# Eleven pairs of seven products in the second input projection

## The reference

```
z = rms_norm(h, norm1_g) @ w_in            # 1024 x 3584: 28 column tiles of 128
cb, cc, ch = split(z[..., :1536], 3)       # convolution, 4 tiles of 128 each
rq, rk, rv, rg = split(z[..., 1536:], 4)   # retention, 4 heads of 128 each
y_conv = group_rms_norm(cb * causal_dwconv3(cc * ch, conv_w), conv_norm_g, 8)
q = rotary(rq); k = rotary(rk) * 128 ** -0.5
o = chunkwise_retention(q, k, v)           # chunks of 128 tokens, a state from chunk to chunk
y_ret = group_rms_norm(o, ret_norm_g, 4) * silu(rg)
h = h + concat([y_conv, y_ret]) @ w_out
```

## Time and profile before

| | |
|---|---|
| median of 3 runs (lowest, highest) | 2289.05 us (2288.67, 2289.07) |
| time of the profiled execution | 2289.21 us |
| its span, first to last instruction | 2287.4 us |
| mean granted clock of PE | 0.998 |
| PE busy | 2270.7 us, 99% |
| DVE busy | 1598.9 us, 70% |
| POOL busy | 1109.2 us, 48% |
| ACT busy | 818.0 us, 36% |

### The profile page before, as it was taken

One profiled execution on the slowest core, in us unless ns is written; L12 is line 12 of the kernel. 1 busy time (PEld: TensorE's weight loads), 2 busy tenths in 40 slices (PEclk: granted clock), 3 DMA queues, 4 the chain that ended last, 5 costly groups with the idle time before them and its releaser, 6 DMA issues.

```text
span 2287.4 us, 32269 instructions
## 1 busy us (share of the span) xinstructions
PE 2270.7 (99%) x10812; PEld 1896.3 (83%) x10812; DVE 1598.9 (70%) x2259; ACT 818.0 (36%) x1336; POOL 1109.2 (48%) x1252
## 2 busy tenths in 40 slices
PE   9999999999999999999999999999999999999998
PEld 7888888888888888888888888888888888888886
DVE  7666666756778777876666666555687877787766
ACT  5233333334634444444430002002453444344432
POOL 4332323234666566656543333443556665666561
PEclk9999999999999999999999999999999999999999
DMA  4110101124264546454312111111335545554553
GB/s 157 37 37 29 34 31 33 33 77 144 92 213 150 181 172 214 147 183 172 120 49 81 38 37 43 43 45 47 103 136 184 194 146 191 183 190 149 194 195 136
DMA packets 56966, 265.40 MB, mean 116 GB/s; under 512 B 6960, under 2 KB 8112, under 8 KB 39472
## 3 DMA queue, kind: packets, MB, share of 16 engines
q1 hardware_dynamic: 56304, 262.12, 33.5%
q10 hardware_dynamic: 576, 2.13, 0.3%
HBM read 206.55 MB, written 57.67 MB: 116 GB/s over the span
## 4 chain that ended last, share of the span: by engine, by line
PE 94%; DVE 3%; DVEq 1%; ACT 1%; issue 0%; DMA 0%; POOL 0%; SPq 0%; ACTq 0%; POOLq 0%
PE prod_ps L752 13%; PE prod_ps L754 13%; PE prod_ps L753 13%; PE prod_ps L1018 8%; PE prod_ps L1019 8%; PE prod_ps L1020 8%; PE side_ps L1018 7%; PE side_ps L1019 7%; PE side_ps L1020 7%; PE side_ps L893 2%; PE side_ps L805 2%; PE side_ps L811 1%; PE side_ps L821 1%; PE side_ps L831 1%; PE side_ps L823 1%; PE prod_ps L1052 1%
## 5 line engine op out<-in xcount | busy, mean ns | idle before, releaser
L752 PE MATMUL prod_ps<-operand_hi,w_hi 128*128 128x512 f32 x1336 | 532.0, 398 | 0.9 <-DVE operand_lo L1452 0.3
L754 PE MATMUL prod_ps<-operand_hi,w_lo 128*128 128x512 f32 x1336 | 521.7, 390 | 0.0
L753 PE MATMUL prod_ps<-operand_lo,w_hi 128*128 128x512 f32 x1336 | 520.3, 389 | 0.0
L579 POOL CAST w_hi<-w_raw 128x1024 fp32r<-128x1024 f32 x81 | 86.7, 1071 | 655.2 <-PE prod_ps L754 630.9
L583 POOL TENSOR_TENSOR w_lo<-w_raw,w_hi 128x256 fp32r<-128x256 f32 x324 | 302.6, 964 | 6.5
L754 PEld LDWEIGHTS prod_ps<-operand_hi,w_lo 128*128 128x128 f32 x1336 | 250.7, 188 | 53.9
L752 PEld LDWEIGHTS prod_ps<-operand_hi,w_hi 128*128 128x128 f32 x1336 | 251.1, 188 | 51.7 <-issue 1.5
L753 PEld LDWEIGHTS prod_ps<-operand_lo,w_hi 128*128 128x128 f32 x1336 | 251.2, 188 | 49.0
L624 POOL TENSOR_TENSOR w_lo<-w_raw,w_hi 128x256 fp32r<-128x256 f32 x168 | 155.7, 947 | 128.2 <-ACT w_hi L2551 127.4
L624 POOL TENSOR_TENSOR w_lo<-w_s,w_hi 128x256 fp32r<-128x256 f32 x168 | 129.7, 775 | 142.8 <-ACT w_more_hi L2559 114.8
L1863 DVE TENSOR_TENSOR x_res<-prod_ps,x_res 128x512 f32<-128x512 f32 x130 | 89.0, 685 | 95.7 <-PE prod_ps L1020 95.6
(11 more groups left out here) (369 smaller groups left out, 5413.3 us busy)
## 6 DMA issues: line engine op xcount, KB each, us to landing
w_raw<-stream SPq DMA_DIRECT2D x202, 512.0 KB, 3.7
x_park<-x_res SPq DMA_DIRECT2D x45, 1024.0 KB, 8.0
x_res<-x_park SPq DMA_DIRECT2D x45, 1024.0 KB, 6.7
swapped<-op_park SPq DMA_DIRECT2D x39, 1024.0 KB, 5.0
op_park<-swapped SPq DMA_DIRECT2D x6, 1024.0 KB, 7.8
x_in<-x_t SPq DMA_DIRECT2D x16, 256.0 KB, 5.5
x_res<-x_t SPq DMA_DIRECT2D x8, 512.0 KB, 4.5
out_t<-x_res SPq DMA_DIRECT2D x16, 256.0 KB, 2.0
```

The costliest lines, as they stand in the source:

```text
L579: nc.gpsimd.tensor_copy(w_hi[:, slot], w_raw[:, slot]).then_inc(high_made, 1)
L752: nc.tensor.matmul(into, w_h, a_h, start=(k == 0), stop=False)
L753: nc.tensor.matmul(into, w_h, a_l, start=False, stop=False)
L754: last = nc.tensor.matmul(into, w_l, a_h, start=False, stop=(k == KT - 1))
```

## The change

Units `U_IN2`+6 to the last of the convolution, 22 of them, are taken in 11 pairs. A pair of units is two column blocks by two halves of tokens. Over inner tiles 0-3 its four outputs are made from seven products of sums (operands B11, B21, B22 and T1 to T4; weights A11, A12, A22 and S1 to S4) instead of eight; over inner tiles 4-7 they are made plainly (`plain`). The first six units stay as they were. All four banks of `prod_ps` serve a pair, in an order that `pair_banks` turns from pair to pair. ACT copies four intermediate values out of PSUM to `in_c`, and DVE adds them (`got`) before it goes on; three of the four evacuations then read `in_c` in SBUF. Slot 0 of the weights holds the part for seven products, slot 1 the plain part.

T2, T3, T4 and the further weight parts take the place of `x_res`. So `x_res` is scaled early (gain on ACT, factor on POOL for tiles 4, 5, 6, 7, 0, 1; tiles 2, 3 on DVE), written to DRAM (`end1_park`, four transfers of 1 MB) and read back at the output projection (eight of 512 KB). The operands T1 to T4 are made on DVE and ACT in heads 0 and 1 and in pair 0. The copies of v, o and back move from DVE to ACT. The retention's loop is written out; its steps stand at named places of the pairs.

```diff
+            def split_paired(j):
+
+                u = U_PAIRED + 2 * j
+                raw, s12_raw = w_raw[:, 0], s12[0]
+
+                def behind(event):
+                    if j:
+                        pool.wait_ge(in_prod, 7 * (j - 1) + event)
+
+                def low(dst, src, high, highs):
+                    pool.wait_ge(in_high, 4 * j + highs)
+                    return nc.gpsimd.tensor_tensor(dst, src, high.bitcast(F32), ALU.subtract)
+
+                def upper(i):
+                    ks = slice(4 * i, 4 * i + 4)
+                    nc.gpsimd.tensor_copy(w_hi[:, 1, ks], w_raw[:, 1, ks]).then_inc(in_up_high, 1)
+                    pool.wait_ge(in_up_high, 2 * j + i + 1)
+                    for ks in (slice(4 * i, 4 * i + 2), slice(4 * i + 2, 4 * i + 4)):
+                        last = nc.gpsimd.tensor_tensor(w_lo[:, 1, ks], w_raw[:, 1, ks], w_hi[:, 1, ks].bitcast(F32),
+                                                       ALU.subtract)
+                    return last
+
+                pool.wait_ge(w_landed[0], u * 8 + 16)
+                if j:
+                    behind(4)
+                else:
+                    pool.wait_ge(prod, 2 * u - 2)
+                nc.gpsimd.tensor_tensor(s12_raw[:, 0:2], raw[:, 4:6], raw[:, 6:8], ALU.add)
+                pool.drain()
+                nc.gpsimd.tensor_tensor(s12_raw[:, 2:4], s12_raw[:, 0:2], raw[:, 0:2], ALU.subtract).then_inc(in_sum, 1)
+                low(w_lo[:, 0, 0:2], raw[:, 0:2], w_hi[:, 0, 0:2], 1).then_inc(in_parts, 1)
+                low(w_lo[:, 0, 2:4], raw[:, 2:4], w_hi[:, 0, 2:4], 1).then_inc(in_parts, 1)
+                low(w_lo[:, 0, 4:6], s12_raw[:, 0:2], w_hi[:, 0, 4:6], 2).then_inc(in_parts, 1)
+                behind(5)
+                if not j:
+                    pool.wait_ge(prod, 2 * u)
+                pool.wait_ge(w_landed[1], u * 8 + 16)
+                upper(0).then_inc(in_parts, 1)
+                behind(6)
+                if not j:
+                    pool.wait_ge(end1_parked[1], 16)
+                nc.gpsimd.tensor_tensor(in_s34[:, 0:2], raw[:, 0:2], raw[:, 4:6], ALU.subtract)
+                nc.gpsimd.tensor_tensor(in_s34[:, 2:4], raw[:, 2:4], s12_raw[:, 2:4], ALU.subtract).then_inc(in_sum, 1)
+                low(w_lo[:, 0, 6:8], s12_raw[:, 2:4], w_hi[:, 0, 6:8], 2).then_inc(in_parts, 1)
+                for ks in (slice(0, 2), slice(2, 4)):
+                    part = low(in_s34_lo[:, ks], in_s34[:, ks], in_more_hi[:, ks], 3)
+                part.then_inc(in_parts, 1)
+                low(in_a22_lo[:], raw[:, 6:8], in_more_hi[:, 4:6], 4).then_inc(w_split, 1)
+                pool.wait_ge(prod, 2 * u)
+                upper(1).then_inc(w_split, 1)
+                pool.sem_inc(high_made, 2)
...
+                part(1)
+                free(n_u)
+                seventh(b_u, A11, B11, True).then_inc(in_prod, 1)
+                part(3)
+                free(n_v)
+                sum_ready(1)
+                seventh(b_v, S1, T1, True).then_inc(in_prod, 1)
+                free(n_w)
+                seventh(b_w, A12, B21, True)
+                then("P2")
+                part(4)
+                plain(b_w, 0, 0, False).then_inc(in_prod, 1)
+                then("c11")
+                copied(1)
+                part(5)
+                sum_ready(2)
+                seventh(b_u, S2, T2, False).then_inc(in_prod, 1)
+                then("P6")
+                free(n_z)
+                plain(b_z, 0, 1, True)
+                part(6)
+                seventh(b_z, S4, B22, False).then_inc(in_prod, 1)
+                then("c12")
+                copied(3)
+                sum_ready(3)
+                seventh(b_u, S3, T3, False).then_inc(in_prod, 1)
+                then("P7")
+                pe.wait_ge(w_split, u + 2)
+                plain(b_v, 1, 1, False).then_inc(in_prod, 1)
+                then("c22")
+                copied(4)
+                sum_ready(4)
+                seventh(b_u, A22, T4, False).then_inc(prod, 2)
+                then("P4")
+                plain(b_u, 1, 0, False).then_inc(prod, 2)
+                then("c21")
...
+            paired(0, {"P2": old(1, "v"), "c11": old(1, "kv"), "c12": old(1, "o")})
+            paired(1, {"c11": new(2, "scores"), "c12": old(1, "back"), "c22": new(2, "k"), "c21": old(2, "v")})
+            paired(2, {"P2": old(2, "kv"), "c12": old(2, "o"), "P4": new(3, "scores")})
+            paired(3, {"P2": old(2, "back"), "c11": new(3, "k"), "c12": old(3, "v"), "c22": old(3, "kv")})
+            paired(4, {"P2": old(3, "o"), "P7": old(3, "back")})
...
+            def got(u, slot, half):
+
+
+                if not (isinstance(u, int) and U_PAIRED <= u < U_OUT2):
+                    wait_prod(u, half)
+                    return bank(slot, half), evac
+                j, odd = divmod(u - U_PAIRED, 2)
+                b_u, b_v, b_w, b_z = (prod_ps[:, n] for n in PAIR_BANKS[j])
+
+                def add(c, src):
+                    nc.vector.tensor_tensor(c[:], src, c[:], ALU.add).then_inc(evac, 1)
+                    dve.drain()
+                    return c[:], in_used
+
+                if not odd and half == 0:
+                    dve.wait_ge(in_copied, 4 * j + 1)
+                    dve.wait_ge(in_prod, 7 * j + 3)
+                    return add(in_c[0], b_w)
+                if not odd:
+                    dve.wait_ge(in_copied, 4 * j + 3)
+                    nc.vector.tensor_tensor(in_c[2][:], in_c[2][:], in_c[1][:], ALU.add)
+                    dve.drain()
+                    dve.wait_ge(in_prod, 7 * j + 5)
+                    return add(in_c[2], b_z)
+                if half == 1:
+                    dve.wait_ge(in_copied, 4 * j + 4)
+                    dve.wait_ge(in_prod, 7 * j + 7)
+                    return add(in_c[3], b_v)
+                dve.wait_ge(prod, 2 * u + 2)
+                return b_u, evac
...
+            def in_combine(op, m, half, other):
+
+                for kk in range(2):
+                    last = nc.vector.scalar_tensor_tensor(
+                        in_raw[op][:, kk], x_res[:, m + kk, tokens(half)], gain[:, G_END1_MIX2, m + kk:m + kk + 1],
+                        in_raw[other][:, kk], ALU.mult, ALU.subtract)
+                last.then_inc(in_t_made, 1)
+
+            def in_low(op, n):
+                dve.wait_ge(in_t_high, n)
+                nc.vector.tensor_tensor(in_lo[op][:], in_raw[op][:], in_hi[op][:].bitcast(F32), ALU.subtract
+                                        ).then_inc(in_t_ready, 1)
+
+            def first_in_sum():
+                dve.wait_ge(in_scaled, 1)
+                in_combine(T1, 0, 1, T1)
+
+            def other_in_sums():
+                dve.wait_ge(in_scaled, 2)
+                in_combine(T3, 2, 1, T3)
+                dve.wait_ge(end1_parked[3], 16)
+                in_combine(T2, 2, 1, T1)
+                dve.drain()
+                in_combine(T4, 2, 0, T2)
...
+            q_half(1, 0)
+            other_in_sums()
+            ret_states(0)
+            q_half(1, 1)
...
+            for u in range(U_PAIRED + 2, U_OUT2 + 2):
+                load_next(u, u % 2)
+            sp.wait_ge(prod, 2 * U_OUT2 - 2)
+            for k in range(KT):
+                sp.dma_start(x_res[:, k], end1_park[k // 2, :, k % 2]).then_inc(x_again[k], 16)
+                if k + 2 < KT:
+                    load_next(U_OUT2 + k + 2, k % 2)
```

## The result

The changed kernel takes 2299.4 us (median of 5, 2298.53 to 2300.3), the kernel before 2288.84 us beside it (median of 5, 2288.32 to 2289.07). The ratio is 1.0041 with a 95% interval of 1.003 to 1.0053: some 10 us slower, and the interval is clear of 1. The forecast was 2292.3 us with a range up to 2299; the time lies 7.1 us above the one and 0.4 us above the other.

A forecast was written before the change was run, and what follows sets the result against it. TensorE, busy 2270.7 of 2287.4 us, was taken as the bound. 2289.2 - 15.0 + 3.9 + 0.3 + 1.5 + 5.0 + 2.8 + 0.3 + 5.0 = 2293.0; 2292.8 against the median, some 0.5 off for catch-up: 2292.3 us, range 2285 to 2299.

The forecast's parts named there:

- Removed: Second input projection on TensorE: eleven pairs of 90 products instead of 96 save 66 products of 0.2267 us, 15.0 us.
- The four places that it names: TensorE waits at head 1's step "o", pair 0, pair 4's step "back" and the output projection's entry.
- Step "o" of head 1: TensorE waits for states because six sums precede VectorE's last state operations: 3.9 us (3.4 to 4.7).
- Back: Pair 4, last head: TensorE waits for the normalisation, behind a gate half on VectorE: 5.0 us (4.1 to 6.5).
- the entry: Output projection start: TensorE waits for GpSimd's split of slot 0, released at A22 of pair 10: 2.8 us (1.5 to 3.6).
- A22 by T4: Pair 0: this product waits for T4's low part from VectorE: 1.5 us (0.8 to 2.5).
- "o" in pair 0: Pair 0: TensorE's step waits for VectorE's states: 0 to 0.6 us, taken as 0.3.
- The rule on two SBUF operands: GpSimd contends with VectorE instructions having two SBUF inputs: gate multiplication 1.22 us beside a split, 0.75 with GpSimd idle.
- The clock: Low-clock stretches behind the waits at head 1, pair 4 and probably the output projection: 2.0, 2.0 and 1.0, 5.0 us.
- a bank wait: Third bank of pairs 7 and 10, freed by VectorE just before it is wanted: 0.3 us (0 to 3).
- rival D: VectorE becomes the bound in the pairs through slower SBUF operations, third bank late: 2301 us, chance 0.21.
- C: Rival: the waits don't come, as VectorE's real order or speed hides them: 2274 to 2283 us, chance 0.07.

The follow-up runs named there:

- e9: The changed kernel with the edits of e8, e6 and e7 together, and q times xi of head 1 behind its scores: 2276.68 us, ratio 0.9942.
- e6: The changed kernel with GpSimd's second pair of residual multiplications put behind the next weight unit: 2298.57 us, ratio 1.004.
- e12: The changed kernel with each 128x1024 GpSimd multiplication of the residual cut into four of 128x256, same places: 2296.41 us, ratio 1.0027.
- e2: The changed kernel with the states of head 0 ahead of the six sums on VectorE: 2298.73 us, ratio 1.0036.
- e4: The changed kernel with the low part of T4 made directly behind that of T3 on VectorE: 2297.21 us, ratio 1.0036.
- e11: The changed kernel itself, unedited, run once more with a second profile: 2299.99 us.
- e7: The changed kernel with the output projection's first weight unit split after S4 of the last pair, not after A22: 2296.35 us, ratio 1.0038.
- e8: The changed kernel with e2, e4, the last head's norm ahead of the third gate tile, and unawaited work put behind qk_ready: 2284.95 us, ratio 0.9984.
- e5: The changed kernel with idle TensorE multiplications in five longer waits, queued ahead of all that these steps wait for: 2292.63 us, ratio 1.0016.

## Why the prediction was wrong in size

**Removed: right.** 66 products of 0.2267 us are 15.0 us; e9, with 1.4 us of waits and no low clock, is 13.1 us under the kernel before.

**The four places that it names: all there, 14.6 us where it has 13.5** (five waits, two of them in pair 0). Step "o" of head 1 took 2.95 us for 3.9, because the six sums took 4.25 us (0.71 each) and not 5.0. "Back" took 4.68 for 5.0, the entry 2.88 for 2.8. A22 by T4 took 3.33 for 1.5, above its range of 0.8 to 2.5, and "o" in pair 0 took 0.77 for 0.3: I priced the operations ahead of it at their length with GpSimd idle (and added them up to 22.7 where they make 22.5), and most that read two SBUF operands were stretched, the T3 and T4 low parts to 1.76 and 1.74 us for 1.2 to 1.3, q times xi to 1.59 for 1.2, and each of the two rotations, whose four operations now read SBUF, to 3.9 and 4.0 for 3.0. GpSimd splits weights beside nearly all of it. From the timeline of DVE:

```profile
1312.01 1.76 DVE L2344 TENSOR_TENSOR in_t_lo<-in_t,in_t_hi 128x1024 fp32r<-128x1024 f32 x1
...
1319.69 1.59 DVE L2396 TENSOR_TENSOR ret_q_xi<-ret_q,ret_rows 128x1024 f32<-128x1024 f32 x1
1321.21 1.74 DVE L2344 TENSOR_TENSOR in_t_lo<-in_t,in_t_hi 128x1024 fp32r<-128x1024 f32 x1
```

The prediction used the rule on two SBUF operands in pair 4 alone, and it held in pair 0 as well.

**A fifth wait was missed: 2.72 us at "scores" of head 0.** This is the step of the prediction that says "By shares nothing becomes the bound" and then walks the waits: it walked head 1 and the pairs but not head 0, and of the early scaling it costed only the parking. In head 0 the change puts 2.2 us of sums in front of "scores", and four of VectorE's operations take 5.2 us more than alone. GpSimd's multiplications of the residual are 128x1024 and take 2.4 to 3.1 us each, and e6 and e12 showed that a VectorE operation on two SBUF operands waits out the running one. The Trainium skill, *SBUF — State Buffer*, section "SBUF: two separate sides", says that the two engines' shared ports are an exclusive lock, held for the whole instruction. The traces agree: 2.89 us beside a whole multiplication, 0.98 beside pieces of a quarter, 0.69 beside none.

**The clock was mis-sized: 5.0 us taken, 8.9 and 7.5 measured** (10.2 and 8.5 with whole windows). I took the cost of one fall from the kernel's start, 2.0 us. Here a stretch of 3.4 us at the low level costs up to 1.7 us and one of 6.8 us up to 3.4, less by what lies in the wait itself. And there were five waits long enough where I counted three. This is the largest part of the error, or as large as the next: 2.5 to 3.9 us of 7.1, against 2.7 of the missed wait and 1.1 of the others. Two small terms nearly cancel: 0.3 for a bank wait that did not come, and 0.5 taken off because a slow stretch lets VectorE catch up, which no run here shows.

**The banks, rival D and the rest.** No wait on a bank and none on a weight part shows in the eleven pairs, so D did not happen; that its time (2301) was the nearest is chance. GpSimd's pieces, the parking and ScalarE's root were hidden as claimed. C's time was out of reach for the kernel as written, but not for the change: e9 has it, with the same products, other orders and one earlier release of a weight slot.

## What to carry to other kernels

A cut in the bound engine's work moves its next requests earlier, and each helper's order must be walked again: not only how much work a helper has, but what stands ahead of the piece that is waited for. Three orders that each removed a wait of 3 to 4.7 us gained 0.7 to 5 us alone (the 0.7 and 2.2 of e2 and e4 are within the scatter), since the wait moved one step on or the clock fell elsewhere; all edits together gained 22.7 us over the changed kernel. In a kernel like this one price a TensorE wait of some 2.7 us or more with the clock behind it, and look at long GpSimd operations beside VectorE's two-operand ones before looking at shares.

## What the runs showed of the hardware

Between 1180 and 1620 us the low level of the clock came in stretches of 3.4 or 6.8 us at 0.50, nothing between, in each of the ten traces that have any. Of the cost, 1.7 or 3.4 us at most, what falls into the wait itself is not paid: the three stretches of 6.8 us in the changed kernel cost 2.8 to 3.0 us. Behind which wait it came was not fixed: two executions of the same kernel, with waits equal within 0.03 us, lost 8.9 and 7.5 us at different places. Over all traces of the stage it came behind the wait of 2.72 us in 6 of 8, behind that of 2.88 in 8 of 9, 2.95 in 5 of 6, 3.33 in 4 of 7 and 4.68 in 7 of 7. In the stage no wait of 2.24 us or less was followed by a fall, but near the start of the kernel 1.94 us (e11, at 8.80) and 1.67 us (e4, at 8.19) were, while the changed kernel kept the clock after 1.77 us at 8.48. The variants with open waits scatter more than e9, which has next to none (2293.7 to 2299.9 us for e7, 2275.8 to 2278.7 for e9), and the scatter goes with the clock: the mean granted clock of the fastest and slowest executions is 0.995 and 0.993 in e7, 0.998 and 0.995 in e8 (2283.3 and 2288.1 us), 0.998 and 0.996 in e5 (2291.1 and 2295.6 us), 0.998 and 0.997 in e9. That is read from single executions and not tested by a run of its own.
